# A decoder block on one core: decay row's chain, two gate pages, the first weight's low parts and the order of the first token tiles

## The reference

```python
h = layer_norm(x, ln0_g, ln0_b)
proj = jnp.einsum('bsd,dn->bsn', h, w_in[i])
(hg_q, hg_f, hg_i, hg_g, fx_q, fx_k, fx_v, fx_f, gate_a, gate_b) = jnp.split(proj, split_at, axis=-1)
y_a = hgrn2_branch(hg_q, hg_f, hg_i, hg_g, lb, hg_norm_g[i])
y_b = fox_branch(fx_q, fx_k, fx_v, fx_f, fox_fb[i])
merged = (jax.nn.sigmoid(gate_a) * jnp.einsum('bsc,cd->bsd', y_a, w_a[i])
          + jax.nn.sigmoid(gate_b) * jnp.einsum('bsc,cd->bsd', y_b, w_b[i]))
```

```python
log_f = jax.nn.log_sigmoid(f_lin.astype(jnp.float32) + f_bias.astype(jnp.float32))
c = jnp.cumsum(log_f.transpose(0, 2, 1), axis=-1)
```

## Time and profile before

| what | us |
|---|---|
| median of 3 runs | 1658.88 |
| lowest and highest | 1657.49, 1660.45 |
| the profiled execution | 1660.29 |
| its span | 1658.5 |

### The profile page before, as it was taken

One profiled execution on the slowest core, in us unless ns is written; L12 is line 12 of the kernel. 1 busy time (PEld: TensorE's weight loads), 2 busy tenths in 40 slices (PEclk: granted clock), 3 DMA queues, 4 the chain that ended last, 5 costly groups with the idle time before them and its releaser, 6 DMA issues.

```text
span 1658.5 us, 20952 instructions
## 1 busy us (share of the span) xinstructions
PE 1605.9 (97%) x7872; PEld 1339.4 (81%) x7872; DVE 1063.9 (64%) x1630; ACT 694.5 (42%) x1084; POOL 657.2 (40%) x467
## 2 busy tenths in 40 slices
PE   5999999999999999999999989999999999999996
PEld 4888888878888788878887868888888887888886
DVE  7648878426777600046516879986666579867977
ACT  3244454317888720021133543545544443333342
POOL 2132221412233243334444398665555422333334
PEclk9999999999999999999999999999999999999999
DMA  8211011101010221111334425464344498868672
GB/s 279 76 52 39 26 37 29 39 26 39 27 52 26 55 73 40 50 51 51 102 112 141 165 100 194 142 240 151 140 149 166 175 321 268 264 197 234 195 213 102
DMA packets 204851, 200.63 MB, mean 121 GB/s; under 512 B 8520, under 2 KB 174664, under 8 KB 202704
## 3 DMA queue, kind: packets, MB, share of 16 engines
q1 hardware_dynamic: 201584, 188.22, 36.3%
q10 hardware_dynamic: 3168, 11.08, 1.7%
HBM read 153.10 MB, written 46.17 MB: 120 GB/s over the span
## 4 chain that ended last, share of the span: by engine, by line
PE 83%; DVE 6%; ACT 4%; issue 3%; POOL 2%; DMA 2%; SPq 0%; ACTq 0%; DVEq 0%; POOLq 0%
PE dense L888 12%; PE dense L878 7%; PE dense L880 7%; PE dense L882 6%; PE dense L1200 3%; PE dense L1201 3%; PE dense L1202 3%; PE dense L1280 3%; PE dense L1282 3%; PE dense L1281 3%; PE mixA L1019 2%; PE mixA L1200 2%; PE mixA L1201 2%; PE mixB L1201 2%; PE mixB L1202 2%
## 5 line engine op out<-in xcount | busy, mean ns | idle before, releaser
L888 PE MATMUL dense<-parts 128*128 128x512 f32 x1008 | 246.7, 396 | 1.3 <-ACT page L1363 1.3
L763 POOL CAST parts<-page 128x1024 fp32r<-128x1024 f32 x55 | 60.7, 1103 | 439.0 <-PE dense L882 197.5
L888 PEld LDWEIGHTS dense<-parts 128*128 128x128 f32 x1008 | 184.3, 188 | 36.9 <-POOL parts L771 1.5
L771 POOL TENSOR_TENSOR parts<-page,parts 128x512 fp32r<-128x512 f32 x132 | 186.9, 1437 | 45.0 <-ACT parts L1618 40.6
L878 PE MATMUL dense<-parts 128*128 128x512 f32 x528 | 183.6, 409 | 2.8 <-DVE parts L2140 1.2
L880 PE MATMUL dense<-parts 128*128 128x512 f32 x528 | 173.9, 391 | 0.0
L882 PE MATMUL dense<-parts 128*128 128x512 f32 x528 | 173.4, 390 | 0.0
L852 POOL TENSOR_TENSOR parts<-page,parts 128x512 fp32r<-128x512 f32 x52 | 89.0, 1736 | 208.1 <-ACT parts L1739 208.1
L814 POOL TENSOR_TENSOR page<-page 128x512 f32<-128x512 f32 x80 | 121.6, 1521 | 65.6 <-PE dense L1202 25.8
L822 POOL TENSOR_TENSOR parts<-page,parts 128x512 fp32r<-128x512 f32 x80 | 114.8, 1437 | 50.6 <-ACT parts L1665 45.5
L1749 ACT CAST parts<-page 128x1024 fp32r<-128x1024 f32 x56 | 58.5, 1052 | 143.9 <-DVE page L2374 121.9
(11 more groups left out here) (256 smaller groups left out, 3856.1 us busy)
## 6 DMA issues: line engine op xcount, KB each, us to landing
page<-in_w_ff SPq DMA_DIRECT2D x104, 512.0 KB, 6.0
page<-act_scratch SPq DMA_DIRECT2D x56, 512.0 KB, 5.7
page<-in_w_in SPq DMA_DIRECT2D x90, 256.0 KB, 3.3
act_scratch<-page SPq DMA_DIRECT2D x16, 1024.0 KB, 3.9
act_scratch<-page SPq DMA_DIRECT2D x16, 768.0 KB, 7.0
page<-in_w_o SPq DMA_DIRECT2D x32, 256.0 KB, 3.1
h_scratch<-page ACTq DMA_DIRECT2D x8, 512.0 KB, 2.8
page<-c_scratch SPq DMA_DIRECT2D x8, 512.0 KB, 5.0
```

The lines of the kernel that those rows point to most:

```text
L771: ins = nc.gpsimd.tensor_tensor(R(lo, at, HALF), F(raw_page(c), at, HALF), R(hi, at, HALF).bitcast(F32), ALU.subtract)
L888: ins = mm(o, wlo if n == 2 else whi, x_, start=first and n == 0, stop=last and n == 2)
```

## The change

Four edits:

- The second half of the decay row's work (ScalarE's exp and log, VectorE's last four steps) moves from ahead of the FoX values into the second of them: on ScalarE it stands ahead of the copy of tile 1, on VectorE behind the low part of tile 1.
- Gates 2 and 6 of branch A exchange pages 31 and 33. The exponential of gate 2 then waits for the scores of the first 56 steps, which read page 33, and not for the transposes of step 62.
- The low parts of the first weight move from VectorE (four instructions of 128x1024) to GpSimd (eight of 128x512), ahead of its loop over the chunks.
- The order of the first token tiles changes. VectorE: statistics and first norm step of tile 1 ahead of the low part of tile 0, its second norm step behind it; then for every tile statistics and norm of t + 1, then the low part of t. ScalarE: the estimate for tile 1 behind the high part of tile 0. TensorE: in every job the next tile is turned behind k-step 2. `norm_apply` is cut into `norm_begin` and `norm_end` for that.

```diff
--- before.py
+++ after.py
@@ -110,7 +110,7 @@
 PG_QS, PG_KS, PG_KL = (50, 51), (52, 53), (33, RAW + 1)
 PG_PTH2, PG_PTL2 = 5, 9
 
-PG_GA = [27, 29, 31, 28, 30, 32, 33, 34]
+PG_GA = [27, 29, 33, 28, 30, 32, 31, 34]
 PG_GB = [35, 36, 37, 38, 39, 40, 41, SPARE]
 PG_YAH, PG_YAL, PG_YBH, PG_YBL = (50, 51, 13, 14), (52, 53, 17, 18), (19, 20, 21, 22), (23, 24, 25, 26)
 PG_M1, PG_M2 = 46, 47
@@ -743,6 +743,13 @@
                     ins.then_inc(qk_lo, 1)
                 pool.wait_ge(qk_lo, NHG + 2 * hh + 2)
 
+            for j in range(4):
+                pool.wait_ge(w0_hi, j + 1)
+                for at in (0, HALF):
+                    ins = nc.gpsimd.tensor_tensor(R(WLO + j, at, HALF), F(PG_W0 + j, at, HALF),
+                                                  R(WHI + j, at, HALF).bitcast(F32), ALU.subtract)
+                ins.then_inc(w0_split, 1)
+
             for c in range(4, C_END):
                 hi, lo = PARTS[c]
                 for hh in {25: (0, 1), 27: (2, 3), 28: (4,), 29: (5,), 30: (6,), 31: (7,)}.get(c, ()):
@@ -979,12 +986,8 @@
 
             turn_tokens(0)
             for t in range(TT):
-                if t >= 2:
-                    turn_tokens(t + 1)
                 pe.wait_ge(h_split, t + 1)
-                value_job("vhg", t, (3, turn_tokens) if t == 1 else None)
-                if t == 0:
-                    turn_tokens(1)
+                value_job("vhg", t, (2, turn_tokens))
 
             for name in (("f", 0), ("q", 0)):
                 for _ in std(name):
@@ -1349,7 +1352,7 @@
                 nc.scalar.copy(R(WHI + j), F(PG_W0 + j)).then_inc(w0_hi, 1)
                 if j == 1:
                     tokens_high(0)
-            rstd_estimate(1)
+                    rstd_estimate(1)
             for t in range(1, TT + 1):
                 if t + 1 < TT:
                     rstd_estimate(t + 1)
@@ -1491,11 +1494,12 @@
             tmp = F(PG_XP)[0:NFX, :]
             done(act, "crow")
             nc.scalar.copy(tmp, out_of("crow")[LOW_AT:LOW_AT + NFX, :]).then_inc(c_low, 1)
-            act.wait_ge(c_abs, 1)
-            own_step(A(tmp, tmp, ACT.Exp, scale=-1.0))
-            A(tmp, tmp, ACT.Ln, bias=1.0).then_inc(c_log, 1)
             for t in range(TT):
                 done(act, "vfx", t)
+                if t == 1:
+                    act.wait_ge(c_abs, 1)
+                    own_step(A(tmp, tmp, ACT.Exp, scale=-1.0))
+                    A(tmp, tmp, ACT.Ln, bias=1.0).then_inc(c_log, 1)
                 if t == TT - 1:
                     act.wait_ge(c_stored, 16)
                 nc.scalar.copy(v_part(t, False, R), out_of("vfx", t)[:, 0:HG].rearrange(
@@ -1508,7 +1512,7 @@
                 if k >= 5:
                     act.wait_ge(qk_lo, NHG + 2 * (6 if k == 5 else 8))
                     if k == 7:
-                        act.wait_ge(p_turned, TURNED[63])
+                        act.wait_ge(qk_done, 8 * 7)
                     neg_exp(G_PAGES[k - 5], gx_exp, "gx", k - 5)
                 elif k % 2 == 0:
                     n = k // 2 + 1
@@ -1842,17 +1846,24 @@
                 then(V.tensor_scalar(work, est, est, hv, ALU.mult, ALU.mult))
                 then(V.tensor_scalar(res, work, 1.5, est, ALU.add, ALU.mult))
 
-            def norm_apply(dst, src, i, g, b, tile):
-
-                res = rstd[:, i, 2:3]
+            def norm_begin(dst, src, i, g, tile):
+
                 dve.wait_ge(var_ready, tile + 1)
                 half_var(i)
                 then(V.scalar_tensor_tensor(out=dst, in0=src, scalar=mv[:, i, 0:1], in1=g,
                                             op0=ALU.subtract, op1=ALU.mult))
+
+            def norm_end(dst, i, b, tile):
+
                 dve.wait_ge(rs_est, tile + 1)
                 newton(i)
-                return V.scalar_tensor_tensor(out=dst, in0=dst, scalar=res, in1=b,
+                return V.scalar_tensor_tensor(out=dst, in0=dst, scalar=rstd[:, i, 2:3], in1=b,
                                               op0=ALU.mult, op1=ALU.add)
+
+            def norm_apply(dst, src, i, g, b, tile):
+
+                norm_begin(dst, src, i, g, tile)
+                return norm_end(dst, i, b, tile)
 
             def low_part(lo_all, hi_all, src, t):
                 cols = slice(t * P, (t + 1) * P)
@@ -1874,22 +1885,15 @@
             tokens_stats(0)
             dve.wait_ge(rows_in, 32)
             tokens_norm(0)
-            for j in range(4):
-                dve.wait_ge(w0_hi, j + 1)
-                V.tensor_tensor(R(WLO + j), F(PG_W0 + j), R(WHI + j).bitcast(F32), ALU.subtract).then_inc(w0_split, 1)
-                if j == 1:
-                    tokens_low(0)
             tokens_stats(1)
-            tokens_norm(1)
+            norm_begin(F(PG_X + 1), F(PG_X + 1), 1, F(PG_G0), 1)
+            tokens_low(0)
+            norm_end(F(PG_X + 1), 1, F(PG_B0), 1).then_inc(h_ready, 1)
             for t in range(1, TT):
                 if t + 1 < TT:
                     tokens_stats(t + 1)
-                if t == 1:
-                    tokens_low(t)
-                if t + 1 < TT:
                     tokens_norm(t + 1)
-                if t > 1:
-                    tokens_low(t)
+                tokens_low(t)
 
             for i in range(2):
                 dve.wait_ge(h_stored[i], 16 * (TT // 2))
@@ -2069,12 +2073,6 @@
                                    op0=ALU.add, op1=ALU.add).then_inc(c_lin, 1)
             dve.wait_ge(c_lin, 1)
             V.scalar_tensor_tensor(out=tmp, in0=z, scalar=-1.0, in1=z, op0=ALU.mult, op1=ALU.max).then_inc(c_abs, 1)
-            dve.wait_ge(c_log, 1)
-            then(V.scalar_tensor_tensor(out=z, in0=z, scalar=0.0, in1=tmp, op0=ALU.min, op1=ALU.subtract))
-            then(V.memset(tmp, 1.0))
-            then(V.tensor_tensor_scan(tmp, tmp, z, 0.0, ALU.mult, ALU.add))
-            V.tensor_scalar(z, tmp, -1.0, None, ALU.mult).then_inc(c_ready, 1)
-
             dve.wait_ge(w_split, C_VFX)
             for t in range(TT):
                 if t in (3, 5):
@@ -2083,6 +2081,12 @@
                 dve.wait_ge(v_ready, TT + t + 1)
                 V.tensor_tensor(v_part(t, True, R), out_of("vfx", t)[:, 0:HG].rearrange("q (n c f) -> q n c f", n=NPAIR, c=2),
                                 v_part(t, False, R).bitcast(F32), ALU.subtract).then_inc(v_split, 1)
+                if t == 1:
+                    dve.wait_ge(c_log, 1)
+                    then(V.scalar_tensor_tensor(out=z, in0=z, scalar=0.0, in1=tmp, op0=ALU.min, op1=ALU.subtract))
+                    then(V.memset(tmp, 1.0))
+                    then(V.tensor_tensor_scan(tmp, tmp, z, 0.0, ALU.mult, ALU.add))
+                    V.tensor_scalar(z, tmp, -1.0, None, ALU.mult).then_inc(c_ready, 1)
 
             blocks = R(PG_PTH2, 0, 6 * 1024).rearrange("q (j n) -> q j n", n=2 * P)
             for G in range(16 * NPAIR + 4):
```

## The result

The changed kernel took 1647.62, 1649.28 and **1651.57 us** (the last is the median over all five executions) against 1660.06 us for the kernel before, timed beside it: ratio **0.9934**, 95% interval 0.9918 to 0.9951, so 11.0 us less (8.1 to 13.6). Its two other executions took 5.7 and 8.6 ms; the comparison leaves them out, and none of the eleven later executions of the same kernel did so. The forecast was 1650.5 us, 8.4 us less. The profiled execution took 1647.62 us.

A forecast was written before the change was run, and what follows sets the result against it. TensorE, busy 97% of the span, was taken as the bound, so only its waits and the slower clock behind them could return. Gains 2.4 + 4.4 + 1.6 = 8.4 us gave 1650.5 us against the median 1658.88; range 1646.3 to 1653.9.

The forecast's parts named there:

- The start: First token tiles: low parts moved to GpSimd and the new order gain 2.4 us, bounds -0.9 and 5.1.
- the term of the lock waits: First token tiles: seven VectorE norm steps each meet a GpSimd step and wait 0.5 to 1.0 us, 5.5 together.
- the turn inside tile 0: Tile 1's eight transposes, now behind k-step 2 of tile 0, take 2.0 us at the lower clock.
- The term for the turn given back: Tile 3's transposes move from ahead of tile 2 to within it, so 1.0 us of the earlier start is lost.
- My lower bound of -0.9 us: First token tiles: each of seven norm steps waits for a whole GpSimd step, 8.8 us in all; gain -0.9 us.
- the upper bound, no contention: First token tiles: without lock waits TensorE alone sets the pace, tile 2 starts at 32.7; gain 5.1 us.
- The decay row: FoX values: moving the row's second half removes TensorE's wait for a low part and its delay; 4.4 us, bounds 3.9 and 4.5.
- The pages: Gate 2 on page 33: its exponential starts 1.65 us earlier, TensorE's 1.3 us wait goes; 1.6 us, bounds 1.3 and 1.65.
- Milder contention: Rival: GpSimd yields or meets fewer steps, start gains 5.1, whole gain 11.1 us, 1647.8 us; chance 0.18.
- Harder contention: Rival: GpSimd slips in twice or a longer gap lowers the clock; start -0.9, gain 5.1, 1653.8 us; chance 0.16.
- Edits that don't do what they say: Rival: another wait stands at the same place; gain 2.9 us, 1656.0 us, within 0.2%; chance 0.07.
- Slower by GpSimd's pairs: Rival: GpSimd's pairs bound tile 0; at 8 us a pair 15.7 us lost against 8.4 gained, 1666.2 us; chance 0.03.

The follow-up runs named there:

- the late first pair: The changed kernel with GpSimd's first pair of low-part steps held until token tile 0 is normed: 1650.62 us against 1660.71 before, ratio 0.9942.
- the doubled pairs: The changed kernel with a second, unused pair of steps ahead of each of GpSimd's pairs: 1661.18 us against 1660.71 before, ratio 1.0009.
- order alone: The kernel before with only the new token-tile order from tile 1 on, weight's low parts left on VectorE: 1659.35 us against 1660.71, ratio 0.9996.
- GpSimd alone: The kernel before with only the first weight's low parts moved to GpSimd, old token-tile order: 1660.95 us, ratio 1.0003.
- the quarter steps: The changed kernel with GpSimd's eight steps of 512 columns cut into sixteen of 256: 1650.26 us against 1659.69 before, ratio 0.9940.

## Why the prediction was right, and where it was off

**The direction and the three parts are shown.** Faster at 0.9934 (forecast 0.9950, with its range from 0.9924 to 0.9970, all against the median shown before). Each of the three parts ran alone, and each gives its own share: start and decay row in timing and trace, the pages in the traces.

**The start: the term of the lock waits was mis-sized.** Forecast 2.4 us, found 4.3 in the profiled trace and 4.1 to 4.4 in the others, counted from the first norm step. The mechanism was right: the PSUM-reading low part loses nothing, the steps with two operands from SBUF wait their turn, GpSimd's run fills without gaps, the first value matmul moves back (18.1 forecast, 17.86 found) and the four pairs end at 24.6 (25.7 forecast). The step that was off is "the seven norm steps wait 5.5 us together by my count": 4.05 us. With 1.45 us less, tile 2's low part ends at 29.9 + 4.05 = 33.95 by the forecast's own working, against 33.57 in the trace (32.36 + 1.21). Tile 2 starts at 33.62 instead of 35.4, 1.8 us of the 1.9 that the start is better. Two smaller terms went the same way, and neither adds to the sum, because VectorE and not TensorE sets tile 2's start: the turn inside tile 0 took 1.0 us and not 2.0 (the clock had risen by 21.84; in two later executions it rose within the turn, which took 1.5 and 1.7 us), and tile 1 started at 26.89, not 28.2. That VectorE sets it shows in two other traces too: with the decay row alone and the pages alone, slow matmuls follow tile 1's wait for 5.3 us where it was 3.7, and the start from the first norm step on is 66.5 us where it was 66.4. The term for the turn given back, 1.0 us, held: tile 2 moved by 5.20, the last copy by 4.27.

The exclusive lock is as the Trainium skill has it (SBUF — State Buffer, section Who interferes with whom: a VectorE instruction with two SBUF inputs and a GpSimd instruction reading SBUF exclude each other). The trace agrees, for GpSimd's casts too (1.04 us alone, 2.04 at 29.32 beside the norm step of 28.37), and adds what the page leaves open: no norm step waited longer than 1.00 us, less than one GpSimd step (1.25 us), so GpSimd never got two in. My lower bound of -0.9 us rested on a whole step at each meeting; the upper bound, no contention, is refuted by every row of the start.

**The decay row: right, with luck in the closeness.** Forecast 4.4, bounds 3.9 and 4.5; found 4.5 in the trace of the change and 4.46 alone, both against the one trace that the forecast was read from. Against the five traces of the old chain it is 3.1 to 6.0. The wait and its end were forecast rightly; that the slower clock behind it costs what it cost in that trace was taken for granted, and it is the part that scatters. The order of events is the forecast's. Tile 1's low part is done at 332.36 + 0.69 = 333.05; with the start's lead of 4.27 that is 337.3 on the old time axis, where I wrote 337.4. The chain's end and tile 2's low part (339.23 to 339.90, so 344.2) are 0.7 us later than my 343.5, while GpSimd's steps of 336.81 stand beside them, and still ahead of the 344.6 at which tile 4 wants it: no wait of TensorE names L2082. Nor does one name the loads behind the decay row in SP's queue, costed at nothing.

**The pages: right in kind, slightly low in size.** Forecast 1.6, bounds 1.3 to 1.65; found 1.75 by the exponential and by the stream behind it, alone. (The 1.97 of the whole change hold 0.22 us that go with the decay row.) The forecast took the exponential's own move, 1.65 us, as the upper bound; it is 1.7 to 1.8 over all the traces. TensorE's own 1.3 us wait went as forecast. In the timeline of TensorE of the kernel before:

```profile
...
579.37 1.06 PE L1099 MATMUL mixB<-ident,page 128*128 128x128 f32 x8 [0.64 <-DVE parts L2121]
...
582.40 0.39 PE L1113 MATMUL dense<-parts 128*128 128x256 f32 x1 [0.58 <-DVE parts L2121]
...
584.42 1.78 PE L888 MATMUL dense<-parts 128*128 128x512 f32 x7
```

the waits for the transposed parts are 0.64 and 0.58 us; in the changed kernel's rows above they are 0.36 and 0.29 (568.95, 571.71). With the pages alone only the first of them shrinks, to 0.37. So TensorE's waits give 1.25 + 0.27 = 1.5 of the 1.75 us; the remaining 0.2 are not in a wait that the view names.

**The sum.** 8.4 forecast, 10.7 in the trace up to the gate, 11.0, 9.1 and 11.0 by the ratios of the three timings of the same kernel. The extra 2.3 is 1.9 of the start, 0.15 of the pages, 0.2 of the wait behind the gate that goes with the decay row, and 0.1 of the decay row, less rounding. The median over all five executions, 1651.57, is only 1.1 us from the forecast, but it is the slowest of the three that the comparison keeps; by the ratio the gain was undersized by about a quarter.

**The rivals.** Milder contention (11.1 us): nearer in size than my forecast: 11.0 by the ratio, and the start's 4.3 lies closer to its 5.1 than to my 2.4; as a mechanism it is half right, for each step did wait, but shorter. Harder contention: refuted for this change, the clock did not fall again and no step waited for two; its other half, a longer gap that brings the lower clock back, came with the late first pair. Edits that don't do what they say: refuted by the missing L2084 and L1363 entries. Slower by GpSimd's pairs: refuted for this change, and shown as a mechanism by the doubled pairs and by the late first pair.

**What stays open.** What tells the 2.06 us wait, which no lower clock followed, from the 2.14 us one was not tried, nor what decides between none, 3 and 6 us of it behind the same wait of 2.9 us. That the down projection's waits scatter because of its weight's loads is argued from ScalarE's waits for them (19.5 to 22.0 us in total, from 7 to 9 waits), not shown.

## What to carry to other kernels

An engine relieved of work gains nothing until the order of the work uses the relief: of two edits that only work together each alone measured 0.0% here, so a part that tests at zero is not thereby useless. When vector work moves to GpSimd, count one lock wait of about half a GpSimd step for each VectorE instruction with two SBUF operands that it runs beside, and give the moved steps a deadline: here the fourth pair ended at 24.62, 0.17 us before TensorE reached the k-step that needs it (24.79), with another 0.53 us of waiting behind the tile as cover, and being 1.8 us later used that up. Where a bottleneck engine's wait hangs on another engine's chain, look at its later waits on the same chain too: here one of two shrank with it. And a wait that one trace prices with a stretch of slower clock behind it should get a range: the same 2.9 us wait cost 3.1 to 6.0 us in five traces.

## What the runs showed of the hardware

In these traces the wait for the lock was never longer than the step that held it, and the two engines alternated: with GpSimd steps of 128x512 (1.25 us alone) the seven meetings cost 1.00, 0.70, 0.45, 0.64, 0.36, 0.80 and 0.10 us, 0.58 on average; the five of them that met GpSimd's own run cost 0.63 on average, and 0.35 with steps of 128x256, at a price of 2.0 us for GpSimd in all. Beside VectorE's norm steps a GpSimd pair takes 3.4 to 3.5 us instead of 2.5, and 4.36 in one case where each half meets a norm step (order alone, 26.75).

TensorE's waits of 2.14 us (first pair late), 2.36 (GpSimd alone, tile 1), 2.83 (before, tile 1) and 3.67 (order alone) were each followed by a stretch at the 1.2 GHz level of about 3 us, two of 3.06 us at tile 1 (decay row alone, pages alone) by one of about 5; the waits of 0.53 and 0.8 us were not, and behind the 2.06 us wait of the quarter steps the clock reads 1.00 and the matmuls take 0.39 us. But the length of the wait does not settle it: of five waits of 2.9 us at the same place of the program, three were followed by about 3 us of it, one by about 6 and one by none.

The column alone can mislead at a start: in the changed kernel it reads 1.00 from 18 to 20 us, while the matmuls there take 0.63 us where they take 0.39 later; with the doubled pairs it reads 1.00 from 24 to 28 us too, where they take 0.63 and the eight transposes of 25.79 take 1.91 instead of 1.03. The duration of one instruction form is the better witness.

One place scatters between executions of one kernel: TensorE's waits for low parts in the down projection were 1.0, 3.3 and 2.9 us in three profiled executions of the changed kernel, whose spans were 1645.7, 1648.5 and 1648.6. That is most of their difference, and more than the pages' whole effect.
